# Expert weights rounded to bf16 in DRAM during the mixers, twelve row buffers, one activation table in attention, copies on the freer engine

## What is computed

```python
# layer 0
y = rmsnorm(h);  z = y @ w_in                                   # 1024 -> 2048
p, q, k, v = z[:512], z[512:1024], z[1024:1536], z[1536:]       # by column
a = (window_mean(p, 2/4/8/16 per group) - p) @ w_pool * scale   # 4 groups of 128
b = chunk_attention(q, k, v, rel_bias)     # 8 heads of 64, own chunk of 64 and 8 before it
h = h + concat(a, b) @ w_out
h = h + moe(rmsnorm(h))
# layer 1
z = gelu(rmsnorm(h) @ w_in + b_in);  u, v = z[:1024], z[1024:]
h = h + (u * (tril(w_s) @ layernorm(v) + b_s)) @ w_out          # blocks of 128 positions
h = h + moe(rmsnorm(h))
out = rmsnorm(h)
# moe: best of 4 groups, best 2 of its 4 experts
out[n] = sum over 2 experts of  w[n,e] * (silu(t @ w_gate[e]) * (t @ w_up[e])) @ w_down[e]
```

## Time and profile before

| | us |
|---|---|
| median of 3 runs | 2552.05 (2547.46 to 2552.96) |
| the profiled execution, its own time | 2554.51 |
| its span, slowest core | 2552.6 (cores 2519.7 to 2552.6) |
| granted TensorE clock of the cores | 0.878 to 0.887 of full speed |
| busy: TensorE / VectorE / ScalarE / GpSimd | 1950.7 / 1276.1 / 1117.7 / 650.5 |

### The profile page before, as it was taken

The page is one execution under the profiler, slowest core; times in us unless marked ns, Lnnn a source line. Parts: engine busy times, 40 slices in busy tenths (PEclk is TensorE's granted clock), DMA queues, the critical chain, the costliest instruction groups (busy, mean ns, idle before and its releaser), DMA issues.

```text
span 2552.6 us, 30819 instructions; the slowest of 8 cores (2519.7 to 2552.6 us)
## 1 busy us (share of the span) xinstructions
PE 1950.7 (76%) x10179; PEld 953.4 (37%) x10374; DVE 1276.1 (50%) x2933; ACT 1117.7 (44%) x1817; POOL 650.5 (25%) x892
## 2 busy tenths in 40 slices
PE   0787888888787874867689959999999566667886
PEld 0333434343342413423334425555555333233343
DVE  2446555554545543434334436666665444435555
ACT  0466585756657471322223343444444133334343
POOL 2002011010101103323233312223223233334443
PEclk9988988888887956989899978999999778888999
DMA  9321111121120467365642152223223926564310
GB/s 227 76 82 50 66 34 67 41 75 50 50 77 15 108 95 137 101 143 137 144 125 98 33 141 100 100 100 100 100 100 100 165 80 131 140 135 130 118 46 1
DMA packets 88229, 243.46 MB, mean 95 GB/s; under 512 B 22360, under 2 KB 31064, under 8 KB 87568
## 3 DMA queue, kind: packets, MB, share of 16 engines
q0 software_dynamic: 57840, 130.65, 23.2%
q1 hardware_dynamic: 30240, 110.83, 13.1%
HBM read 516.19 MB, written 94.50 MB: 239 GB/s over the span
## 4 chain that ended last, share of the span: by engine, by line
PE 36%; DVE 19%; ACT 18%; DMA 14%; issue 5%; POOL 5%; another core or an unknown queue 3%; POOLq 1%; DVEq 0%; SPq 0%; ACTq 0%
PE psum L520 13%; DMA arena<-H,arena 9%; PE psum L849 6%; PE psum L826 6%; PE psum L621 4%; ACT L1105 3%; PE psum L1062 2%; PE psum L1098 2%; ACT arena L1071 2%; ACT L1071 2%; DMA out<-arena 2%; POOL arena L657 2%; DVE arena L1270 2%; ACT arena L1105 2%
## 5 line engine op out<-in xcount | busy, mean ns | idle before, releaser
L520 PE MATMUL psum<-arena 128*128 128x512 bf16 x2961 | 773.8, 406 | 57.6 <-ACT arena L585 13.8
L826 PE MATMUL psum<-arena 128*128 x1714 | 437.2, 392 | 40.3 <-ACT arena L838 19.0
L520 PEld LDWEIGHTS psum<-arena 128*128 128x128 bf16 x3072 | 301.7, 104 | 428.1 <-issue 89.1
L510 POOL TENSOR_SCALAR arena<-arena 128x1 f32<-128x1 f32 x215 | 53.2, 247 | 993.8 <-ACT arena L600 510.1
L826 PEld LDWEIGHTS psum<-arena 128*128 128x128 bf16 x1760 | 175.0, 100 | 252.4 <-issue 83.9
L849 PE MATMUL psum<-arena 128*128 x852 | 244.1, 420 | 2.4 <-issue 0.7
L853 DVE TENSOR_TENSOR arena<-psum,arena 128x1024 f32<-128x1024 f32 x110 | 134.6, 1224 | 207.4 <-PE psum L849 207.4
L829 ACT ACTIVATE arena<-psum 128x256 f32<-128x256 f32 x220 | 83.3, 379 | 325.3 <-PE psum L826 325.2
L799 DVE SCALAR_TENSOR_TENSOR arena<-arena 128x1024 bf16<-128x1024 f32 x110 | 140.8, 1282 | 160.8 <-DMA arena<-H,arena 156.7
L1071 ACT ACTIVATE arena<-psum 128x512 bf16<-128x512 f32 (+1 forms) x304 | 169.2, 586 | 93.6 <-PE psum L1062 92.2
L600 ACT ACTIVATE arena<-arena 128x1024 bf16<-128x1024 f32 x64 | 67.6, 1056 | 309.1 <-DVE arena L596 299.3
(11 more groups left out here) (169 smaller groups left out, 2502.7 us busy)
## 6 DMA issues: line engine op xcount, KB each, us to landing
arena<-wmoe POOLq DMA_DIRECT2D x114, 1536.0 KB, 25.0
arena<-x SPq DMA_DIRECT2D x64, 512.0 KB, 3.6
H<-arena SPq DMA_DIRECT2D x64, 512.0 KB, 2.8
arena<-H SPq DMA_DIRECT2D x64, 512.0 KB, 3.8
arena<-ab_w_in POOLq DMA_DIRECT2D x4, 1024.0 KB, 55.5
arena<-sgu_w_in POOLq DMA_DIRECT2D x4, 1024.0 KB, 10.6
TBL<-arena SPq DMA_DIRECT2D x2, 1536.0 KB, 35.9
arena<-gvec SPq DMA_DIRECT2D x5, 512.0 KB, 4.4
```

Source lines behind the costliest of these rows:

```text
L520: P.add("pe", lambda e, kc=kc: e.matmul(bank(b), lhsT=lhs(kc), rhs=rhs(kc), start=(kc == 0), stop=(kc == n - 1)), reads=reads(kc), writes= ...
L826: return e.matmul(bank(b), lhsT=tT[i % 2][:, kc, :], rhs=wslice(e, i, x_, kc * 1024), start=(kc == 0), stop=(kc == 7))
```

## The change

- **Weights.** A DRAM tensor WB of bf16 is added. `convert` (POOL, DRAM to DRAM) rounds one expert; three per stage of `attention` for layer 0, two per stage of mixer 1 for layer 1. `expert_load` and `load_step` now read WB and are issued by SP.
- **MoE.** 12 row buffers instead of 6, six of them in memory that is free by then.
- **Attention.** The table set that has both Ln and Exp is loaded once at the start. V's ones stand on the other side for odd heads, so that a pair of heads fills the two halves of the partitions; Ln reads PSUM, one Exp and two multiplies serve the pair, and the copy to SBUF is gone. Output banks are 2, 3, 4, score banks 0, 1, 7 (7 shared with the projections, which have 5, 6, 7).
- **Copies.** `copy` gives the scheduler a choice of ScalarE or VectorE (for a small one VectorE or GpSimd); `either` a choice of VectorE or GpSimd for the window sums, the bias multiplies and the memsets of attention.
- **Scheduler.** New durations in `estimate`, a DMA clock for each issuing engine.
- **Start.** `poolw` has a group of its own; the bias tables, `w_out`, the zeroing of TBL and the ones of V for stages 1 and 2 come after the first `stage1` (`start_rest`).

```diff
     if eng == "act":
-        return ((172 if ps else 224) + sz) / 1.2, 60
+        return ((172 if ps else 224) + sz) / 1.2 + 20 + (200 if "accum_out" in k else 0), 60
     if eng == "dve":
-        return ((120 if ps else 62) + sz) / 0.96, 60
-    return 400 + sz * 1.1, 60
+        return (60 + 0.4 * sz if n == "memset" else 150 + 1.05 * sz), 60
+    if k.get("op") == ALU.pow:
+        return 450 + 180 * sz, 60
+    return (150 + 0.8 * sz if n == "memset" else 250 + 1.1 * sz), 60
...
+                if op.alts:
+                    f = st + op.alts[e][1]
+                    if any(max(free_t[q], ready[op]) + op.alts[q][1] < f for q in op.alts if q != e):
+                        continue
...
-                dma_t[0] = max(dma_t[0], st + op.dur) + op.lat / 250.0
-                op.fin = dma_t[0] + 2000.0
+                dma_t[e] = max(dma_t[e], st + op.dur) + op.lat / 180.0
+                op.fin = dma_t[e] + 2000.0
...
+        def convert(l, e_, extra):
+            r = slice((l * 16 + e_) * 128, (l * 16 + e_ + 1) * 128)
+            P.add("pool", lambda e: e.dma_start(out=WB[r, :], in_=wmoe[r, :], max_dma_last_dim=8192),
+                  writes=[("wb", l, e_)], grp=P.group("cv%d_%d" % (l, e_)), extra=extra, t=(1000, 3100000))
...
         def expert_load(l, e_, slot, key):
-            P.add("pool", lambda e: e.dma_start(out=dst, in_=wmoe[(l * 16 + e_) * 128:(l * 16 + e_ + 1) * 128, :], max_dma_last_dim=8192),
-                  writes=[key], grp=P.group("slot%d" % slot[1]))
+            P.add("sync", lambda e: e.dma_start(out=dst, in_=WB[(l * 16 + e_) * 128:(l * 16 + e_ + 1) * 128, :]),
+                  reads=[("wb", l, e_)], writes=[key], grp=P.group("slot%d" % slot[1]), t=(70, 1600000))
...
-            NH = 6
-            hr = [work.buf([128, D], key=k("hr", i)) for i in range(NH)]
+            NH = 12
+            hr = [(work if i < 6 else more).buf([128, D], key=k("hr", i)) for i in range(NH)]
...
-                    return e.dma_start(out=W8[:, bass.ds(d, 2 * EW)].bitcast(BF16), in_=wmoe[l * 2048:(l + 1) * 2048, :][bass.ds(r, 128), :], cond=c, max_dma_last_dim=8192)
-                loads[i] = P.add("pool", fn, reads=["regs"], writes=[("lds", i % 8)], grp=P.group("ld%d" % (i % 8)), extra=[after] if after else [], t=(2000, 30000))
+                    return e.dma_start(out=W8[:, bass.ds(d, 2 * EW)].bitcast(BF16), in_=WB[l * 2048:(l + 1) * 2048, :][bass.ds(r, 128), :], cond=c)
+                loads[i] = P.add("sync", fn, reads=["regs"] + [("wb", l, q) for q in range(6, 16)], writes=[("lds", i % 8)], grp=P.group("ld%d" % (i % 8)),
+                                 extra=[after] if after else [], t=(1500, 100000))
...
-        NPB = 4; SB = [(0,), (1,), (2,)]; OB = [(3,), (4,)]
+        NPB = 4; SB = [(0,), (1,), (7,)]; OB = [(2,), (3,), (4,)]
...
+        P.add("act", lambda e: e.preload_act_table_set("natural_log_exp_and_others"), t=(1300, 0))
...
-        cload(poolw, pool_w.rearrange("g c d -> c g d"), "poolw", "pool")
+        cload(poolw, pool_w.rearrange("g c d -> c g d"), "poolw", "pool", grp=P.group("constp2"))
...
-                if last:
-                    o = OS[hh % 2]; ok = ("AOS", hh % 2); d = atT[s % 2][po:po + 64, j, :]
-                    P.add("dve", lambda e: e.tensor_copy(o, bank(ob)), reads=[PS(ob)], writes=[ok])
-                    P.add("act", lambda e: e.activation(out=Rn[0:64, :], in_=o[64:128, :], func=AF.Ln), reads=[ok], writes=["ARn"])
-                    P.add("act", lambda e: e.activation(out=Rn[0:64, :], in_=Rn[0:64, :], func=AF.Exp, scale=-1.0), reads=["ARn"], writes=["ARn"])
-                    P.add("dve", lambda e: e.tensor_tensor(out=d, in0=o[0:64, :], in1=Rn[0:64, :], op=ALU.mult), reads=[ok, "ARn"], writes=[("Aat", s % 2, j)])
+                if last and hh % 2:
+                    oe, oo = otile[hh - 1], otile[hh]
+                    R = Rn[j % 2]; ke, ko = ("AR", j % 2, 0), ("AR", j % 2, 1)
+                    P.add("act", lambda e: e.activation(out=R[0:64, :], in_=bank(oe)[64:128, :], func=AF.Ln), reads=[oe], writes=[ke])
+                    P.add("act", lambda e: e.activation(out=R[64:128, :], in_=bank(oo)[0:64, :], func=AF.Ln), reads=[oo], writes=[ko])
+                    P.add("act", lambda e: e.activation(out=R, in_=R, func=AF.Exp, scale=-1.0), reads=[ke, ko], writes=[ke, ko])
+                    for o, q, kk in ((oe, 0, ke), (oo, 64, ko)):
+                        P.add("dve", lambda e: e.tensor_tensor(out=atT[s % 2][q:q + 64, j, :], in0=bank(o)[q:q + 64, :], in1=R[q:q + 64, :], op=ALU.mult),
+                              reads=[o, kk], writes=[("Aat", s % 2, j, q)])
...
+            if s == 0:
+                start_rest()
+            conv = [P.all[-1]]
             attention(s)
+            for q in range(3 * s, min(3 * s + 3, 16)):
+                convert(0, q, conv)
...
             run_all(norms1(s), vstage(s), ustage(s))
+            for q in range(2 * s, 2 * s + 2):
+                convert(1, q, [P.all[-1]] if q % 2 == 0 else [])
```

133 lines of the change are left out of this document (76 added, 57 removed).

## The result

The changed kernel takes **2316.15 us** (median of four runs, 2313.98 to 2317.8) against 2552.51 us in the same session; the ratio is 0.9071, 95% interval [0.9047, 0.9095]. The forecast was 2207 us in a range from 2120 to 2330: the sign and the range hold, and 236 us were gained where the sum had 345. The profiled execution took 2316.2 us, its span on core 6 is 2314.3 us. In some executions, of the kernel before too, the cores of one die show a lower granted clock and take longer (the kernel before once took 2639.24 us, with 0.80 to 0.82 on cores 0 to 3 and 0.88 to 0.89 on the others); these are left out of all medians and ranges here.

A forecast was written before the change was run, and what follows sets the result against it. No engine was busy throughout, so bounds were taken by stage: TensorE in mixer 1, table loads in attention, gather waits in the MoEs. Terms 30 + 140 + 25 + 5 + 70 + 80 - 5 = 345 us off 2552 gave 2207 us, range 2120 to 2330.

The forecast's parts named there:

- The start: Start of the kernel: transposes no longer wait for `poolw` and loads move later; 30 us gained, ends 15 and 41.
- About 7 MB of it is moved behind the first stage: Start: of some 15 MB in flight about 7 MB moves later, so `w_in` should be complete near 38 us.
- Converts, 5 us in mixer 1: Mixers: sixteen converts in each, hidden by prefetched x blocks; 5 us charged to mixer 1, ends 10 gained and 40 lost.
- 131.5 + 20.5 removed: Attention: activation-table loads taken off the path, 131.5 us from 111 to 880 us and 20.5 us in the last attention.
- I take 140, near the upper, because the clock is lowest, 0.63, where TensorE is busy least: Attention, 111 to 880 us: 140 us gained, as TensorE's clock rises once table loads go; ends 75 and 154.
- rival (a): Attention: TensorE at its old clock takes ScalarE's place as limit; kernel 2285 us, chance 0.20.
- Copies and multiplies on the freer engine: Attention: copies and window sums on the freer engine, with new scheduler durations; nothing counted.
- rival (d): Attention: GpSimd's multiplies far dearer than the scheduler believes; at 4.1 us each the kernel takes 2580 us, chance 0.05.
- End of mixer 0: Store and load at mixer 0's end, last two 21.6 us; 5 us gained, ends 20 gained and 15 lost.
- The MoEs: Both MoEs: waits for gathered rows go with twelve buffers; 70 us gained in MoE 0, 80 in MoE 1.
- Rival (b): MoEs: wait for expert weights in place of rows, 6 us at each of 20 loads; 2327 us, chance 0.12.
- The table stays swapped (c): Attention: each Exp still brings its own table set, 64 loads, 82 us; kernel 2289 us, chance 0.05.

The follow-up runs named there:

- the fourth run: Changed kernel with first-stage converts tied before the moved loads, layer 1's converts all waiting for their stage, and bias multiplies on VectorE: 2306 us.
- the run with either engine: Changed kernel with three converts per mixer 0 stage, one per mixer 1 stage; bias multiplies still allowed on GpSimd at the changed kernel's price: 2248 us.

## Why the prediction was right or wrong

That the time lies in the range is partly luck. The largest miss, the start, is of a kind that no rival had, and it met errors of the other sign.

**The start: wrong, 114 us.** The step "About 7 MB of it is moved behind the first stage" was right for the loads that move: the first transposes start near 21 us where they started at 71.00. It missed what the change adds there. The converts were costed under a step of their own as sixteen in each mixer; that half of layer 1's had an empty dependency list, and so the start of the program as their place, stands in the diff and was not followed into the schedule. Held back, the start ends at 172.5 us, 24 us earlier than before the change, and without any convert at 161.1 us, 36 us earlier. The table alone gives 16 of these, so some 8 and 20 us are left for the step that the sum had at 30 (an estimate; no run has the moved loads alone).

**Converts, 5 us in mixer 1: right in sum, by luck.** The sum meant sixteen converts there; the changed kernel has eight. The prediction gave the cover, residual and x blocks loaded ahead, and the price without it, 7 us a convert. Mixer 1 takes 435.7 and 436.5 us in the two kernels without converts, 449.7 with the eight that are left there, 1.7 us each, and 543.9 with sixteen, 6.7 us each: near the price without cover, on the slowest pair of cores, and 476 us on the other six (mean). In mixer 0 the sum charged nothing for converts; without them it takes 651.7 us in place of 676.3, so the sixteen of layer 0 cost 25 us. The term was checked against an average of the DMA share; the limit was the store of one block before the load of the next.

**Attention: the mechanism right, the size made of errors that partly cancel.** The table loads were on the path nearly in full: alone, they give 115 us in mixer 0, 16 in the start and 140 in the kernel, against 131.5 + 20.5 removed. TensorE's share rose to the 91% that the sum took. The step that failed is "I take 140, near the upper, because the clock is lowest, 0.63, where TensorE is busy least": the clock stayed at 0.85, between its two levels of 1.2 and 2.4 GHz, and mixer 0 gained 120 us where the sum had 145. The clock is rival (a)'s, the gain is not: (a) had 87 us for all eight attentions.

Two costs that the sum put at nothing stand against a gain that it had too small. Without converts mixer 0 takes 651.7 us, 145 less than before, at a clock of 0.87; with the multiplies on VectorE as well 615.3 us, 181 less, at 0.91. That is 66 us below the 681.2 of the table alone, where the sum had 17 for Ln and Exp and nothing for copies and new durations; which of these edits gives it no run separates.

Small matmuls did hold the clock: it is 1.00 in two stages of 82 and 85 us in the fourth run. Part of what keeps it down in the changed kernel goes with GpSimd's share of the multiplies: 36 to 44 us by three pairs of runs. It is not all, since the run with the table alone has 0.86 without any multiply on GpSimd; the rest of the cause is open.

**Copies and multiplies on the freer engine: put at nothing, 36 to 44 us.** The prediction's "price near the memset" was 0.93 ns an element, and the third that may move was to cost what it costs now. The third was exact (112 of 312). On GpSimd a 128x256 multiply has a mean of 726 ns in the changed kernel against 442 on VectorE, a 128x128 one 629 against 324; so rival (d)'s place was right and its 4.1 us a multiply was not. The Trainium skill's GPSIMD Engine Reference, section Engine selection, says about twice slower with two inputs, and the trace has 1.6 and 1.9. From that page the prediction estimated 37 us; the run with either engine was 36 us slower, but through TensorE's clock and not through the multiplies' own length, so the agreement is luck.

**End of mixer 0: right.** 21.6 us were forecast for the last store and load; they take 15.23 and 5.37 us in the chain of the changed kernel, 20.6. As forecast, four of the six expert loads are issued early, at 856 to 859 us, and the last two at 904.55 and 904.98 us, ahead of the store.

```profile
911.14 15.23 DMA H<-arena
926.39 5.37 DMA arena<-x
```

**The MoEs: right in size; the smaller loads count for more than the buffers.** 155 us forecast with the end of mixer 0, 179.5 measured. Gather waits vanish as forecast, and the cause named in the prediction, gathers late "whenever an expert load shares the DMA engines", fits: with six buffers the half-size loads cut the wait from 150.6 to 61.9 us, though they also left GpSimd's queue. Bf16 experts are worth 26 + 69 us in a kernel with twelve buffers, twelve buffers 25 + 0 us in a kernel with bf16 experts (slowest cores). So in MoE 1 it was the load; in MoE 0 each of the two, without the other, already gives 60 of the 86 us over the kernel before (with the other edits of the change in both). Rival (b) did not come: no engine of the changed kernel's profile waits for a load of expert weights. Whether the queue counts by itself was not tried, since the run with loads as before changes queue and size together (bf16 loads on GpSimd's queue would tell); by the Trainium skill's DMA: Bandwidth & Descriptors, section Issuing engines are not separate DMA queues, the change of queue would save issuing time only. No run here shows it.

**The table stays swapped (c)**: no, by the table run.

## What to carry to other kernels

A list scheduler like this one places a transfer without dependencies at the start of the program; before costing prefetched work, find the instruction that it is tied to and ask what shares that stretch. Cost a group of background transfers by the shortest cover among the chains that they slow (here a store that must land before a load into the same buffer), one transfer at a time: here the first of a stage was hidden and the second cost 13.5 us. Where TensorE is the bound, work moved to a slower engine can be paid in TensorE's clock as well as in waits, so compare TensorE's busy time for the same matmuls. And a part that comes out at its forecast can be two errors: runs that take the costs away one by one show the size of each.

## What the runs showed of the hardware beyond that

Issuing can take long when much is in flight: the second zero fill's issue held SP's queue for 59.55 us in the changed kernel and for 7.10 us with eight converts fewer under way, and the next x load's issue for 59.00 and 5.24 us (80.30 with three converts more). What stood behind them on that queue was issued later too.

With two converts a stage in mixer 1 one pair of neighbouring cores was slow at a time: in one execution cores 6 and 7 took 2335 and 2339 us, in other executions of the same kernel the pairs were 0 and 1 (2332, 2327) or 4 and 5 (2331, 2335), with the other cores between 2221 and 2295 us. What the pair shares no run here tells.

TensorE's clock can stay low under load: in the changed kernel it was 1.00 from 553 to 563 us, with TensorE busy for 9.60 of 10 us, then 0.50 to 0.97, and from 583 to 618 us it was 0.50, its lower level, while TensorE was busy for 3.5 to 5.0 of each 5 us. From 618 to 623 us it was 0.91. What brings it back was not settled.
